# Eight gate groups instead of five computed inside the sparse attention of a two-block transformer kernel, with their sigmoid split between ScalarE and VectorE

## The reference, cut to what matters

```python
def first_block(x, mem, positions, g_mix, w_in, b_gate, ...):
    h = rmsnorm(x, g_mix)
    (q_s, k_s, v_s, q_d, k_d, v_d, q_i, k_i, w_i, q_m, gate_logits) = split(h @ w_in)
    o_swa = sliding_window_attention(rope(q_s), rope(k_s), v_s, sinks)
    o_dsa = dsa_attention(rope(q_d), rope(k_d), v_d, rope(q_i), rope(k_i), w_i * idx_scale)
    o_mem = memory_cross_attention(q_m, mem_k, mem_v)
    gates = sigmoid(gate_logits + b_gate).reshape(B, S, 3, D_MODEL)
    merged = (gates[0] * (o_swa @ w_proj_swa) + gates[1] * (o_dsa @ w_proj_dsa)
              + gates[2] * (o_mem @ w_proj_mem))
    x = x + merged @ w_out
    ...                                   # MLP; then the second block

def dsa_attention(q, k, v, q_idx, k_idx, w_idx):      # 4 heads, blocks of 128 queries
    iscore = sum over 4 index heads of relu(q_idx . k_idx) * w_idx, causal
    _, sel = top_k(iscore, 256)
    s = softmax(q . k[sel] * HEAD_DIM ** -0.5)
    return s @ v[sel]
```

## Time and profile before

| | |
|---|---|
| median of 3 runs | 2705.92 us (2702.24 to 2711.68) |
| the profiled execution's own time | 2707.32 us |
| its span | 2705.5 us |
| granted TensorE clock, mean | 0.969 |
| PE busy | 2504.8 us, 93% |
| DVE busy | 1582.6 us, 58% |
| ACT busy | 1222.1 us, 45% |
| POOL busy | 838.9 us, 31% |

### The profile page before, as it was taken

The page is one execution under the profiler, slowest core; times in us unless marked ns, Lnnn a source line. Parts: engine busy times, 40 slices in busy tenths (PEclk is TensorE's granted clock), DMA queues, the critical chain, the costliest instruction groups (busy, mean ns, idle before and its releaser), DMA issues.

```text
span 2705.5 us, 32753 instructions
## 1 busy us (share of the span) xinstructions
PE 2504.8 (93%) x11852; PEld 2037.0 (75%) x11852; DVE 1582.6 (58%) x2792; ACT 1222.1 (45%) x2238; POOL 838.9 (31%) x740
## 2 busy tenths in 40 slices
PE   4997899999899899999999999998598999999997
PEld 4765778886677677877888886887586888878886
DVE  5347459995463687876445753345647444455666
ACT  6146347747312544544333453234426555543343
POOL 0222432221210265654252400004003656514242
PEclk9998999999999899999999998999798999999999
DMA  4102123324162167777854532222232444396444
GB/s 157 46 16 77 44 64 93 102 98 147 60 199 101 71 202 221 223 225 266 265 185 141 168 109 66 83 86 71 105 131 80 150 155 154 125 339 198 135 157 155
DMA packets 190131, 369.82 MB, mean 137 GB/s; under 512 B 13692, under 2 KB 58372, under 8 KB 189716
## 3 DMA queue, kind: packets, MB, share of 16 engines
q1 hardware_dynamic: 177620, 340.46, 38.4%
q10 hardware_dynamic: 8064, 14.68, 1.4%
q0 software_dynamic: 4288, 12.60, 1.4%
HBM read 266.95 MB, written 100.74 MB: 136 GB/s over the span
## 4 chain that ended last, share of the span: by engine, by line
PE 75%; DVE 10%; DMA 5%; ACT 5%; issue 3%; POOL 1%; SPq 0%; DVEq 0%; ACTq 0%; POOLq 0%
PE bank L2624 7%; PE bank L2625 7%; PE bank L2626 7%; PE bank L2242 7%; PE bank L2244 7%; PE bank L2243 7%; PE bank L2597 5%; PE bank L2598 5%; PE bank L2599 5%; PE bank L2419 3%; PE bank L2420 3%; PE bank L2421 3%; DMA ada<-in_w_ada 2%; DVE ada_sum L1891 2%; PE bank L2339 1%
## 5 line engine op out<-in xcount | busy, mean ns | idle before, releaser
L2597 PE MATMUL bank<-hq_hi,wq_hi 128*128 128x512 f32 x896 | 354.8, 396 | 17.8 <-DVE hq_lo L1899 12.2
L2624 PE MATMUL bank<-ring_b_hi,ring_a_hi 128*128 128x512 f32 x896 | 350.8, 392 | 5.5 <-DVE hidden L1879 5.0
L2598 PE MATMUL bank<-hq_lo,wq_hi 128*128 128x512 f32 x896 | 352.5, 393 | 0.0
L2599 PE MATMUL bank<-hq_hi,wq_lo 128*128 128x512 f32 x896 | 352.3, 393 | 0.0
L2625 PE MATMUL bank<-ring_b_lo,ring_a_hi 128*128 128x512 f32 x896 | 350.3, 391 | 0.0
L2626 PE MATMUL bank<-ring_b_hi,ring_a_lo 128*128 128x512 f32 x896 | 350.1, 391 | 0.0
L1991 DVE TENSOR_TENSOR ring_a_lo<-a_raw,ring_a_hi 128x1024 fp32r<-128x1024 f32 x112 | 153.6, 1371 | 227.1 <-ACT ring_a_hi L1275 226.9
L1275 ACT ACTIVATE ring_a_hi<-a_raw 128x1024 fp32r<-128x1024 f32 x112 | 118.8, 1061 | 334.0 <-PE bank L2626 315.7
L2597 PEld LDWEIGHTS bank<-hq_hi,wq_hi 128*128 128x128 f32 x896 | 170.4, 190 | 57.2 <-DVE hq_lo L1899 18.8
L1838 DVE TENSOR_TENSOR wq_lo<-unit_raw,wq_hi 128x512 fp32r<-128x512 f32 x160 | 159.6, 1003 | 85.3 <-ACT wq_hi L1141 83.4
L2624 PEld LDWEIGHTS bank<-ring_b_hi,ring_a_hi 128*128 128x128 f32 x896 | 169.2, 189 | 41.9 <-DVE hidden L1879 5.9
(11 more groups left out here) (446 smaller groups left out, 5572.6 us busy)
## 6 DMA issues: line engine op xcount, KB each, us to landing
a_raw<-hidden_scratch SPq DMA_DIRECT2D x112, 512.0 KB, 3.3
hidden_scratch<-hidden SPq DMA_DIRECT2D x32, 1024.0 KB, 5.1
w_raw<-in_w_in SPq DMA_DIRECT2D x104, 256.0 KB, 2.8
ada<-in_w_ada SPq DMA_DIRECT2D x96, 256.0 KB, 3.0
hidden_scratch<-hidden SPq DMA_DIRECT2D x32, 768.0 KB, 4.3
unit_raw<-in_w_mlp_in SPq DMA_DIRECT2D x16, 1024.0 KB, 8.4
b_raw<-in_w_mlp_out SPq DMA_DIRECT2D x32, 512.0 KB, 4.5
unit_raw<-in_w_ff SPq DMA_DIRECT2D x16, 1024.0 KB, 5.4
```

The lines of the kernel that those rows point to most:

```text
L2597: mm(o, lh[:, q, :], rh[:, q, :], start=(fresh and q == 0), stop=False, skip_group_check=True)
L2598: mm(o, lh[:, q, :], rl[:, q, :], start=False, stop=False, skip_group_check=True)
L2599: l = mm(o, ll[:, q, :], rh[:, q, :], start=False, stop=(q == 3), skip_group_check=True)
L2624: mm(o, ra_hi[r][:, e, js], rb_hi[r][:, e, :], start=(fresh and v == 0 and e == 0), stop=False, skip_group_check=True)
```

## The change: what it does

1. `HELD` goes from 43 to 40: all eight groups of the last gate chunk are held. Inside the search ScalarE now does 0.75 groups a step instead of 0.9.
2. Two tables, `AHEAD` and `BEHIND`, say how many of the now 32 slices TensorE has behind it ahead of and after the transposes of each step; `GATE_AT` says in which step ScalarE evacuates each held group.
3. The held groups' sigmoid is made as 1 / (1 + exp(-x)): ScalarE does the Exp with a negated bias, VectorE adds 1 and takes the reciprocal of 128x512 values (`held_gate`), and ScalarE issues the store two steps after its Exp (`gate_store`), just ahead of the next held Exp.
4. `bit_f`, `bit_i` and `keep` lie in PSUM bank 7 instead of SBUF; the three flags of the last step get a small SBUF tile `tie`. TensorE waits for the first selection before its first scores.
5. VectorE scales unit v-1 ahead of the low part instead of behind it, and `held_gate` stands between the two.
6. The second half of the projection's weight splits on ScalarE is at step 12 instead of 14.

```diff
+        nbg = misc("neg_gate_bias", [P, 4])
-        keep = misc("keep", [P, 6], i32)
+        tie = misc("tie", [P, 6])
...
+        bit_f = XB[3][:, 0:32]
+        bit_i, keep = [XB[3][:, o:o + n].bitcast(i32) for o, n in ((32, 32), (64, 6))]
...
-        HELD = 43
+        HELD = 40
...
-        SLICE_AT = [range(0, 4)] + [range(2 * v + 2, 2 * v + 4) for v in range(1, 9)]
+        AHEAD = (4, 8, 12, 16, 20, 22, 24, 28, 32)
+        BEHIND = (6, 10, 14, 17, 20, 23, 26, 29, 32)
+        GATE_AT = {0: 40, 1: 41, 2: 42, 3: 43, 4: 44, 6: 45, 7: 46, 8: 47}
...
                 act.wait_ge(group_done, GG + n + 1)
                 if n >= 2:
                     act.wait_ge(g_out[r], 16 * (n // 2))
-                A_(o[:, :], bank[gate_bank(n)][:, :], ACT.Sigmoid, bias=cols[:, c_bgate + f:c_bgate + f + 1])\
-                    .then_inc(group_free, 1)
-                act.wait_ge(group_free, GG + n + 1)
-                act.dma_start(gates_d[f * P:(f + 1) * P, h * 512:(h + 1) * 512], o[:, :]).then_inc(g_out[r], 16)
+                if n >= HELD:
+                    A_(o[:, :], bank[gate_bank(n)][:, :], ACT.Exp, scale=-1.0, bias=nbg[:, f - 20:f - 19])\
+                        .then_inc(group_free, 1)
+                else:
+                    A_(o[:, :], bank[n % 4][:, :], ACT.Sigmoid, bias=cols[:, c_bgate + f:c_bgate + f + 1])\
+                        .then_inc(group_free, 1)
+                    gate_store(n)
...
+            def gate_store(n):
+                r, (f, h) = n % 2, gate_tile(n)
+                o = (gstage if 16 <= n < HELD else gearly)[r]
+                act.wait_ge(group_free, GG + n + 1)
+                if n >= HELD:
+                    act.wait_ge(g_one, n - HELD + 1)
+                act.dma_start(gates_d[f * P:(f + 1) * P, h * 512:(h + 1) * 512], o[:, :]).then_inc(g_out[r], 16)
...
-                for n in range(6 + 9 * k // 10, 6 + 9 * (k + 1) // 10):
+                for n in range(6 + 3 * k // 4, 6 + 3 * (k + 1) // 4):
                     gate_out(n)
...
-                if v <= 8 and v % 2 == 0:
-                    gate_out(HELD + v // 2)
-                if v in (10, 14):
+                if v - 2 in GATE_AT:
+                    gate_store(GATE_AT[v - 2])
+                if v in GATE_AT:
+                    gate_out(GATE_AT[v])
+                if v in (10, 12):
...
+            def held_gate(n):
+                o = gearly[n % 2][:, :]
+                dve.wait_ge(group_free, GG + n + 1)
+                link(tsc(o, o, 1.0, None, ALU.add))
+                nc.vector.reciprocal(o, o).then_inc(g_one, 1)
...
                 if v < 16:
                     dsa_masked(v)
+                if 1 <= v < 17:
+                    dsa_normalized(v - 1)
+                if v - 1 in GATE_AT:
+                    held_gate(GATE_AT[v - 1])
                 if v >= 4 and v % 2 == 0:
...
-                if 1 <= v < 17:
-                    dsa_normalized(v - 1)
...
-                    pe.wait_ge(group_free, GG + n - (0 if n > HELD else 3))
+                    pe.wait_ge(group_free, GG + (n if n >= HELD else n - 3))
...
             pe.wait_ge(is_s, len(ISC))
+            pe.wait_ge(sel_done, 1)
             dsa_scores(0)
             for v in range(18):
                 if v < 15:
                     dsa_scores(v + 1)
                 if v <= 8:
-                    for i in SLICE_AT[v][:len(SLICE_AT[v]) - 1]:
+                    for i in range(BEHIND[v - 1] if v else 0, AHEAD[v]):
                         held_gates(i)
...
                 if v <= 8:
-                    held_gates(SLICE_AT[v][-1])
+                    for i in range(AHEAD[v], BEHIND[v]):
+                        held_gates(i)
```

More of the change, by code:

```diff
@@ L157, in build @@
         cmpj = at("cmpj", [P, D], mybir.dt.bfloat16, t3 + 10240)
-        bit_f = at("bit_f", [P, 32], f32, t3 + 12288)
-        bit_i = at("bit_i", [P, 32], i32, t3 + 12416)
         pd = [at(f"dsa_probs{i}", [P, D], f32, s2 + 4096 * i if i < 3 else s3 + 10240) for i in range(4)]
@@ L264, in build @@
         sel_done, sel_neg = sem("sel_done"), sem("sel_neg")
+        g_one = sem("held_gate")
         ada_in, ada_s, ada_mm, ada_e, ada_ok = [sem("ada_in0"), sem("ada_in1")], sem("ada_sum"), sem("ada_mm"), sem("ada_e"), sem("ada_ok")
@@ L1094, in _ @@
                 sign_counts(k)
-                for n in range(6 + 9 * k // 10, 6 + 9 * (k + 1) // 10):
+                for n in range(6 + 3 * k // 4, 6 + 3 * (k + 1) // 4):
                     gate_out(n)
-            for n in range(34, HELD):
+            for n in range(30, HELD):
                 gate_out(n)
-                if n >= 40:
-                    negated(2 * n - 78)
-                    negated(2 * n - 77)
-            act.wait_ge(g_out[0], 16 * 22)
-            act.wait_ge(g_out[1], 16 * 21)
+                if n >= 34:
+                    negated(n - 32)
+            act.wait_ge(g_out[0], 16 * 20)
+            act.wait_ge(g_out[1], 16 * 20)
             for v in range(18):
@@ L1658, in _ @@
             link(nc.vector.memset(cand[:, :], 0))
+            link(tsc(nbg[:, :], cols[:, c_bgate + 20:c_bgate + 24], -1.0, None, ALU.mult))
             dve.sem_inc(tk_cand, 1)
@@ L1692, in _ @@
                 dve.wait_ge(g_out[i], 16 * 8)
-            above, more, less = bit_f[:, 0:2], bit_f[:, 2:4], bit_f[:, 4:6]
+            above, more, less = tie[:, 0:2], tie[:, 2:4], tie[:, 4:6]
             for i, b in enumerate(SHARED):
```

## The result

The changed kernel takes 2724.1 us (median of 5 runs, 2721.3 to 2732.6), the kernel before 2706.7 (5 runs). The ratio is 1.0074, with a 95% interval of 1.0059 to 1.0089: slower by some 20 us (the medians lie 17.4 apart). The profiled execution took 2723.0 us, with a span of 2721.2 (before 2705.5).

The account below looks back on a forecast made before the run. The prediction took TensorE as the bound, without gaps in search and selection. Added waits of 20 + 9.5 - 1.7 = 27.8 us took the median from 2705.9 to 2733.7 us; range 2725 to 2742, down to 2718 for 8 in 10.

Parts of the forecast that it names:

- the shorter search is worth nothing by itself: Search and selection end 14.7 us earlier, but three groups (16.3 us of TensorE) only move into the sparse attention: zero gain.
- The stall beside GpSimd: In the search, VectorE's small instructions are lengthened where GpSimd's `w_lo` runs, 10.9 us in all; taken as gone.
- Steps 0 to 8: In the sparse attention up to step 8, TensorE's added waits at held groups cost 20 us.
- The bank waits: Steps 1, 2, 3, 6, 7: held groups share bank 3, so TensorE waits for evacuation, 1.45 us each, 7.3 in all.
- The issue of a store ahead of an evacuation: `gate_store` takes ScalarE 0.4 us ahead of the evacuation; on TensorE's path in steps 2, 3, 6: 1.2 us.
- The waits for landings in steps 2, 3 and 4: Evacuating group n waits until the store of group n-2 has landed: 1.7, 8.3 and 1.8 us.
- At the same distance: Step 3: group 41's store meets the `attended(0)` loads as the earlier store did, about 1.4 us behind, landing in 8.7 us.
- Steps 9 and 10: Steps 8 to 10: group 45's store landing, copies, and VectorE's reciprocal ahead of its mask make TensorE wait, net +9.5 us.
- The end: End of sparse attention: earlier scaling removes a 2.84 us TensorE wait, 1.1 given back for the weight splits; net -1.7 us.
- Rival 1: Stores in steps 3 and 8 also land in about 2 us, missing the loads: 2720.4 us; chance 0.12.
- Rival 2: VectorE was the bound, and sparse attention has TensorE room for three more groups: 2691.2 us; chance 0.03.
- Rival 3: VectorE's search stall beside GpSimd stays despite one operand in PSUM, only 3.8 us gained there: 2743.2 us; chance 0.05.

Follow-up runs that it names:

- both edits: Changed kernel with four staging buffers for held groups instead of two, and each held group ending behind the transposes, the next beginning a step later: 2699.3 us, ratio 0.9976.
- the runs on the tables: Kernel before with search tables and kept candidates in PSUM, first scores behind first selection: 2706.7 us; changed kernel with them back in SBUF: 2736.1 us.

## Why the prediction was right or wrong

**That the shorter search is worth nothing by itself**: right, and shown from both sides. The tables in PSUM alone change nothing, and VectorE's gain of some 11 us comes back as 11.6 us more waiting for ScalarE; with all held groups free of waits, three more of them cost exactly their 16.3 us inside the stage and save them ahead of it. The version with eight held groups and both edits gains 6.5 us, the kernel before with the scaling first and the splits at step 12, and five held groups, gains 6.8. So holding eight groups gains nothing even where it costs nothing.

**The stall beside GpSimd**: right; 0.17 us with one operand in PSUM, 0.28 and 0.40 without. In the changed kernel L1699, with one operand in PSUM, takes 0.17 us at 440.67 while GpSimd's L751 runs from 439.79 to 441.08; before, L1686 with both in SBUF took 1.20 beside L747. That one operand in PSUM ends the stall was my assumption: no row of before shows it, and the runs on the tables do. I took 14.7 us for the whole; it was 16.9.

**Steps 0 to 8, forecast 20**: measured 20.7, which is in part luck, since errors cancel.
- The bank waits were sized rightly: 7.3 forecast, and the version with four buffers, which has nothing else there, lies 7.8 above before. The idle time is only 1.00 to 1.31 us each, but each wait also costs 0.25 us of overlap: before, the slice behind transposes of 0.38 us begins 0.13 us after them.
- The issue of a store ahead of an evacuation, 1.2 us in my sum, costs nothing: it stands in the timeline between two copies that ScalarE does anyway.
- The waits for landings in steps 2, 3 and 4, forecast 1.7 + 8.3 + 1.8, were 2.4 + 5.7 + 1.3 us: 9.4 instead of 11.8. The landing in step 3 took 6.0 us instead of 8.7. "At the same distance" was a false step: the two-step delay puts the store 0.44 us behind SyncE's load and not 1.4. But the store issued later shows that the distance accounts for a small part of the difference; the rest is open.
- In their place came what I had only put into the range: TensorE at the lower clock behind the waits of 3.63 and 6.95 us (4.47 us for 12 matmuls instead of 3.03, 2.93 for 6 instead of 1.65, and the product and scores behind them), 3.3 us.

**Steps 9 and 10, forecast 9.5**: measured 6.4. This term was sized 3.1 us too high. The store of group 45 went 0.94 us behind the loads and landed in 6.7 us instead of 8.8; TensorE waited 3.72 + 0.92 for it and the copies instead of 6.6 + 1.9. The reciprocal was sized rightly, 3.353 us against 3.35 (of the bounds that I gave for it, 5.4 is an estimate from its 157 ns for 2 columns and 178 for 4 before, 10.5 ns a column; 0.6 lies between the 484 ns of the earlier trace rows and the 680 of L1789 at 512 columns; the -2.1 and +2.4 us don't follow from them). Its wait was 1.46 us and not 2.7; 0.9 of the difference is hidden behind TensorE's own product ahead of it, which took 1.98 us at the lower clock and not 1.09. The four waits are 6.8 us, less the 2.3 of before 4.5; the remaining 1.9 of the 6.4 is mostly that clock.

**The end, forecast -1.7**: measured -5.6. The 2.8 us of the wait went, 2.7 by the rows. The 1.1 that I gave back for the splits did not come. And 2.7 us of lower clock went, which my sum leaves out: 1.2 of them stood behind the wait that the new order removes, 1.5 behind the wait of 2.79 us ahead of it, which the move of the splits cuts to 0.71.

**The sum**: 20.7 + 6.4 - 5.6 = 21.5 against 27.8; the median 2724.1 instead of 2733.7. The mechanism was right; the two long landings were sized too high, by 4.8 us together, and the end's gain too low, since the clock was taken at nothing. No run shows the 3 us that the range has for the clock; they show 3.3 us lost to it in steps 0 to 8, most of 1.9 in steps 9 and 10, and 2.7 gained at the end. Two signs of the forecast did not come: about 10 us at step 3's evacuation (6.95) and 6 us or more in step 9 (3.72). Rival 1 (landings of 2 us) was wrong in its reason, as the loads do delay the stores, and near in its time, 2720.4, for another. Rival 2 fell with the two runs on the tables. Rival 3 was near in its price: 9.5, and the tables put back cost 10.6, of which 4.5 lie in the search.

## What to carry to other kernels

A queue that is ruled by one bank and two staging buffers is moved beside other work cheaply only if its end and its next beginning have that work between them: in steps 0 to 10 the same eight groups cost 27 us as they stood, 7 with two slices moved, 9 with four buffers, and nothing with both. Before counting on an evacuation, ask what its target buffer waits for, and what large loads are issued at that signal. And a shorter stage on one engine is worth at most what the engine beside it has as gaps, here 0.85 us.

## What the runs showed of the hardware

- A store of 256 KB that takes 2.0 us alone takes 6.0, 6.7 and 7.2 us when it is issued 0.44, 0.85 and 1.56 us behind loads of 3 MB on another queue, and still 6.3 when 6.4 us behind them; 1.4 us ahead of them it takes 2.0. At one distance (0.94 us) two versions show 6.7 and 7.1, and the kernel before 8.7 and 8.8 at 1.4 and 1.3 us, so the distance alone doesn't set it.
- TensorE's clock followed the gaps, but not strictly. Behind waits for the bank of up to 1.3 us 12 matmuls always took 3.00 to 3.06 us. Behind nine waits of 2.4 to 4.6 us they took 4.2 to 5.5 us in eight cases, at a granted clock of 0.50 to 0.68, and 3.02 at 1.00 in one, where the wait was 2.51. One wait of 2.18 us cost no clock, and one of 2.74 us none in the six matmuls behind it. In the sparse attention's second half the same waits came with either level: 1.82 us, 2.8 us (0.56 granted behind it before, 1.00 with the scaling first), and 1.60 with 0.70 behind it. So a wait of 2.4 to 4 us mostly cost another 1.2 to 1.6 us here.
- RECIPROCAL on VectorE takes 3.353 us for 128x512 values, eight times within 2 ns. With 203 ns for 8 columns and 353 for 32 I estimate 0.15 us and 6.26 ns a column.
